# A hybrid mLSTM / attention / MoE step on one core: first projection in two feature halves, context blocks modulated first, one gate wait placed later, one modulation load issued sooner

## The reference

```python
def ada_mod(cvec, w_ada, b_ada):
    m = jax.nn.silu(cvec) @ w_ada + b_ada
    return jnp.split(m[:, None, :], 6, axis=-1)
...
sh1, sc1, g1, sh2, sc2, g2 = ada_mod(c, w_ada[l], b_ada[l])
h = rmsnorm(xs, norm_mix[l]) * (1.0 + sc1) + sh1
q_m, k_m, v_m, o_m, gates, q_d, k_d, v_d = project(h, w_in[l], b_gate[l])
```

## Time and profile before

| | us |
|---|---|
| runs | 775.79, 778.3, 778.33 |
| median | 778.3 |
| profiled execution | 777.91 |
| its span (first to last instruction) | 776.1 |
| TensorE busy in it | 677.3 |
| VectorE busy | 342.4 |
| ScalarE busy | 174.6 |
| GpSimd busy | 103.1 |

### The profile page before, as it was taken

The page is one execution under the profiler, slowest core; times in us unless marked ns, Lnnn a source line. Parts: engine busy times, 40 slices in busy tenths (PEclk is TensorE's granted clock), DMA queues, the critical chain, the costliest instruction groups (busy, mean ns, idle before and its releaser), DMA issues.

```text
span 776.1 us, 7589 instructions
## 1 busy us (share of the span) xinstructions
PE 677.3 (87%) x2660; PEld 364.4 (47%) x2660; DVE 342.4 (44%) x737; ACT 174.6 (23%) x418; POOL 103.1 (13%) x135
## 2 busy tenths in 40 slices
PE   3899999799999999995889989992999999999910
PEld 1344474245555565543667545552544444444400
DVE  2254263131455524468888175667111202111157
ACT  5000200001222111112677412122011211121133
POOL 1222000031101111002451100002111001110040
PEclk9879999999999999998999998996899999999955
DMA  8997423903130130304000386001599999999273
GB/s 292 388 346 256 169 96 105 356 2 136 41 124 14 54 110 14 109 0 164 0 1 1 137 299 269 28 27 61 180 343 359 338 355 356 356 368 346 87 284 136
DMA packets 63027, 137.88 MB, mean 178 GB/s; under 512 B 4647, under 2 KB 11167, under 8 KB 62997
## 3 DMA queue, kind: packets, MB, share of 16 engines
q1 hardware_dynamic: 53064, 112.43, 40.8%
q0 software_dynamic: 5248, 15.63, 5.6%
q10 hardware_dynamic: 4684, 9.44, 3.1%
HBM read 122.70 MB, written 14.74 MB: 177 GB/s over the span
## 4 chain that ended last, share of the span: by engine, by line
PE 75%; DVE 9%; DMA 6%; issue 4%; SPq 3%; ACT 2%; DVEq 0%; POOLq 0%; POOL 0%; ACTq 0%
PE PS L1458 25%; PE PS L1766 14%; PE PS L1644 7%; PE PS L1781 7%; PE PS L1450 5%; DMA PR<-in_w_ada 3%; PE PS L1489 2%; PE PS L1759 1%; PE PS L1633 1%; DVE PR L975 1%; DMA PR<-scratch_mod 1%; PE PS L1563 1%; PE PS L1537 1%; DVE stat L1104 1%; SPq L406 1%
## 5 line engine op out<-in xcount | busy, mean ns | idle before, releaser
L1458 PE MATMUL PS<-RING,hT 128*128 128x512 f32 x480 | 215.8, 598 | 1.3 <-DVE hT L931 1.3
L1458 PEld LDWEIGHTS PS<-RING,hT 128*128 128x128 f32 x480 | 88.7, 192 | 102.7 <-issue 102.2
L1766 PE MATMUL PS<-PR,RING 128*128 128x512 f32 x256 | 113.8, 598 | 0.1
L1644 PE MATMUL PS<-RING,hT 128*128 128x512 f32 x160 | 74.1, 616 | 0.0
L1766 PEld LDWEIGHTS PS<-PR,RING 128*128 128x128 f32 x256 | 47.8, 192 | 55.6 <-issue 53.8
L1781 PE MATMUL PS<-PR,RING 128*128 128x512 f32 x128 | 57.6, 592 | 0.0
L1644 PEld LDWEIGHTS PS<-RING,hT 128*128 128x128 f32 x160 | 30.4, 198 | 33.6 <-issue 33.5
L1319 DVE TENSOR_TENSOR RING<-RING,PS 128x256 f32<-128x256 f32 x16 | 6.7, 422 | 77.8 <-ACT RING L846 77.8
L1314 DVE COPY RING<-PS 128x512 f32<-128x512 f32 x32 | 20.6, 686 | 45.7 <-PE PS L1759 45.2
L1781 PEld LDWEIGHTS PS<-PR,RING 128*128 128x128 f32 x128 | 23.7, 190 | 26.8 <-issue 26.8
L1450 PE MATMUL PS<-hT,RING 128*128 128x512 f32 (+3 forms) x128 | 35.4, 435 | 0.0
(11 more groups left out here) (317 smaller groups left out, 901.7 us busy)
## 6 DMA issues: line engine op xcount, KB each, us to landing
PR<-in_w_gate_up SPq DMA_DIRECT2D x16, 2048.0 KB, 10.5
PR<-in_w_ada SPq DMA_DIRECT2D x20, 1024.0 KB, 13.3
PR<-in_w_down SPq DMA_DIRECT2D x16, 1024.0 KB, 12.5
RING<-in_w_in SPq DMA_DIRECT2D x14, 1024.0 KB, 7.4
scratch_y<-RING ACTq DMA_DIRECT2D x16, 512.0 KB, 7.8
RING<-in_w_ada SPq DMA_DIRECT2D x4, 1024.0 KB, 13.0
RING<-in_w_out SPq DMA_DIRECT2D x4, 1024.0 KB, 6.2
TMP<-scratch_gfr SPq DMA_DIRECT2D x10, 256.0 KB, 4.9
```

Source lines behind the costliest of these rows:

```text
L1458: last = mm(PS[:, m % 2, :], hTv[:, k, t * P:(t + 1) * P], ring[:, ci % 2, k, :], start=(k == 0), stop=(k == KD - 1))
L1644: last = mm(PS[:, i % 4, :], hTv[:, k, t * P:(t + 1) * P], ring[:, (WOUT + q) % 2, k, :], start=(k == 0), stop=(k == KD - 1))
L1766: last = mm(PS[:, 4 + b, :], xgT[:, b, k, :], gub[b][:, k, :], start=(k == 0), stop=(k == KD - 1))
```

## The change

Four things are altered, all in the first part of the program.

1. **Loads.** SP issues the `w_ada` blocks in the order 0, 2, then the first half (features 0 to 511) of the first `w_in` chunk, then blocks 1 and 3, and then the second half of that chunk. Block 1 lies in ring slot 1, block 3 in `TMP`. The ring's chunk 1 ("mq") waits for `ada(1)`.
2. **Order of the projection.** When blocks 0 and 2 are through, VectorE modulates the first four feature blocks, context columns first (`modulate1(0)`), and TensorE runs the first halves of all five "mk" tiles in five PSUM banks (`FIRST_BANK`), with `ada(1)`, `ada(3)` and their columns between them. `modulate1(1)` follows, and the loop over m then runs only the second halves of the first five tiles.
3. **Gate rows.** VectorE's wait for `gate_split`, and the operation that reads the rows, stand behind the second "mk" tile's copy and no longer ahead of the loop.
4. **Late modulation.** Block 9 is loaded right after the store of the gate rows, one chunk sooner.

The diff, cut to its core:

```diff
-CHUNKS = ([("ada", n * 512) for n in range(2)] + [(w, OFF[w]) for w in WIN_ORDER]
-          + [("out", 0), ("out", 512)])
-ADA1, WIN0, WOUT = 0, 2, 9
+CHUNKS = [(w, OFF[w]) for w in WIN_ORDER] + [("out", 0), ("out", 512)]
+WOUT = 7
+FIRST_BANK = (2, 3, 0, 1, 5)
...
-    ada_late = [PR[:, 4096 * i:4096 * (i + 1)].rearrange("p (k n) -> p k n", k=KD) for i in range(2)]
+    ada_w1 = [v.rearrange("p (k n) -> p k n", k=KD) for v in (PR[:, 0:4096], RING[:, 4096:8192], PR[:, 4096:8192],
+                                                              TMP[:, 6676:10772])]
...
-    MB_AFTER = {5: (0, 1), 6: (2, 3), 7: (4, 5, 6), 8: (7, 8, 9)}
+    MB_AFTER = {3: (0, 1), 4: (2, 3), 5: (4, 5, 6), 6: (7, 8, 9)}
...
+        def load_chunk(ci, halves_=(0, 1)):
             kind, col = CHUNKS[ci]
             w = w_dram.get(kind, a["w_in"][0]).rearrange("(h k p) n -> h p k n", h=2, p=P)
-            for hf in range(2):
+            for hf in halves_:
...
-        load_chunk(0)
-        load_chunk(1)
         w_late = a["w_ada"][0].rearrange("(h k p) n -> h p k n", h=2, p=P)
-        for i in range(2):
+
+        def load_ada1(n_):
+            done = (late_in[0], None, late_in[1], ada3_in)[n_]
             for hf in range(2):
-                sp.dma_start(ada_late[i][:, 4 * hf:4 * hf + 4, :],
-                             w_late[hf, :, :, (2 + i) * 512:(3 + i) * 512]).then_inc(late_in[i], 16)
+                sp.dma_start(ada_w1[n_][:, 4 * hf:4 * hf + 4, :], w_late[hf, :, :, n_ * 512:(n_ + 1) * 512]
+                             ).then_inc(half_in[2 + hf] if n_ == 1 else done, 16)
+
+        load_ada1(0)
+        load_ada1(2)
+        load_chunk(0, (0,))
+        load_ada1(1)
+        load_ada1(3)
+        load_chunk(0, (1,))
...
-        for ci in range(2, len(CHUNKS)):
-            kind2, col2 = CHUNKS[ci - 2]
-            if kind2 == "ada":
-                sp.wait_ge(ada_done, col2 // 512 + 1)
+        for ci in range(1, len(CHUNKS)):
+            if ci == 1:
+                sp.wait_ge(ada_done, 3)
             else:
-                sp.wait_ge(mm_done, NT * (WIN_ORDER.index(kind2) + 1))
+                sp.wait_ge(mm_done, NT * (ci - 1))
             load_chunk(ci)
-            if ci == 3:
+            if ci == 1:
                 for n_ in range(4, 8):
                     load_ada2(n_)
-            if ci == 4:
+            if ci == 2:
                 load_ada2(8)
                 sp.wait_ge(gate_step, 2)
                 sp.dma_start(scratch["gfr"], gf.rearrange("p d t -> p (d t)")).then_inc(gf_stored, 16)
-            if ci == 5:
-                for n_ in range(9, 12):
+                load_ada2(9)
+            if ci == 3:
+                for n_ in range(10, 12):
...
-            src = PS[:, m % 2, :]
+            src = PS[:, FIRST_BANK[m] if m < NT else m % 2, :]
...
-        V.memset(gzero, 0.0)
...
-        for n_ in range(4):
-            dve.wait_ge(ada_done, n_ + 1)
-            V.tensor_copy(adp[0:ROWS4 - 1, n_, :], PS[0:ROWS4 - 1, 4 + n_ % 2, :]).then_inc(ada_row, 1)
-        dve.wait_ge(adacol_T, 4)
-        V.tensor_copy(modc[:, 0:8, :], PS[:, 6, 0:16].rearrange("p (k c) -> p k c", c=2))
-        step(V.scalar_tensor_tensor(modc[:, 8:16, :], PS[:, 6, 16:32].rearrange("p (k c) -> p k c", c=2), 1.0,
-                                    cols[:, 16:24].unsqueeze(2).broadcast_to([P, KD, 2]), ALU.add, ALU.mult))
-
-        dve.wait_ge(hraw_a, NT)
-        dve.wait_ge(hraw_v, NT)
-        for k in range(KD):
+        def modulate1(hf):
+
+            for n_ in (hf, 2 + hf):
+                dve.wait_ge(ada_done, 2 * hf + n_ // 2 + 1)
+                V.tensor_copy(adp[0:ROWS4 - 1, n_, :], PS[0:ROWS4 - 1, 4, :]).then_inc(ada_row, 1)
+            ks = slice(4 * hf, 4 * hf + 4)
+            dve.wait_ge(adacol_T, 2 * hf + 2)
+            V.tensor_copy(modc[:, ks, :], PS[:, 6, 8 * hf:8 * hf + 8].rearrange("p (k c) -> p k c", c=2))
+            step(V.scalar_tensor_tensor(modc[:, 8 + 4 * hf:12 + 4 * hf, :],
+                                        PS[:, 6, 16 + 8 * hf:24 + 8 * hf].rearrange("p (k c) -> p k c", c=2), 1.0,
+                                        cols[:, 16 + 4 * hf:20 + 4 * hf].unsqueeze(2).broadcast_to([P, 4, 2]), ALU.add, ALU.mult))
+            if hf == 0:
+                dve.wait_ge(hraw_a, NT)
+                dve.wait_ge(hraw_v, NT)
             for c, (lo, hi) in enumerate(((0, CTX), (CTX, T))):
-                last = V.tensor_scalar(hTv[:, k, lo:hi], hTv[:, k, lo:hi], modc[:, 8 + k, c:c + 1], modc[:, k, c:c + 1],
-                                       ALU.mult, ALU.add)
-            last.then_inc(h_ready, 1)
+                for k in range(4 * hf, 4 * hf + 4):
+                    V.tensor_scalar(hTv[:, k, lo:hi], hTv[:, k, lo:hi], modc[:, 8 + k, c:c + 1], modc[:, k, c:c + 1],
+                                    ALU.mult, ALU.add).then_inc(h_ready, 1)
+
+        modulate1(0)
+        modulate1(1)
+        V.memset(gzero, 0.0)
...
-        dve.wait_ge(gate_split, 64)
-        step(V.scalar_tensor_tensor(ee, gf, -1.0, gf, ALU.mult, ALU.min))
-        dve.sem_inc(gate_step, 1)
...
+            if w == "mk" and t == 1:
+                dve.wait_ge(gate_split, 64)
+                step(V.scalar_tensor_tensor(ee, gf, -1.0, gf, ALU.mult, ALU.min))
+                dve.sem_inc(gate_step, 1)
...
-        ada(0, ADA1)
         xn_T(2)
         xn_T(3)
-        ada(1, ADA1 + 1)
+        ada(0, 0)
         xn_T(4)
         pe.wait_ge(early_loaded, 48)
-        ada_cols(0)
-        ada(2, ADA1 + 2)
-        ada_cols(1)
-        ada(3, ADA1 + 3)
-        ada_cols(2)
-        ada_cols(3)
+        ada_cols(0, 0)
+        ada(2, 1)
+        ada_cols(2, 1)
 
         def gates():
             pe.wait_ge(early_loaded, 48)
+            pe.wait_ge(h_ready, 16)
...
-            ci = WIN0 + c
-            if m >= 2 and hf == 0:
+            ci = c
+            bank = FIRST_BANK[m] if m < NT else m % 2
+            if m >= NT and hf == 0:
                 pe.wait_ge(mm_evac, m - 1)
+            if m < 4 and hf == 0:
+                pe.wait_ge(hraw_a, NT)
+                pe.wait_ge(hraw_v, NT)
...
-                if m == 0:
-                    pe.wait_ge(h_ready, k + 1)
-                last = mm(PS[:, m % 2, :], hTv[:, k, t * P:(t + 1) * P], ring[:, ci % 2, k, :],
+                if m < 2:
+                    pe.wait_ge(h_ready, 8 * hf + 4 * m + k % 4 + 1)
+                last = mm(PS[:, bank, :], hTv[:, k, t * P:(t + 1) * P], ring[:, ci % 2, k, :],
...
+        proj(0, 0)
+        proj(1, 0)
+        ada(1, 2)
+        proj(2, 0)
+        ada_cols(1, 2)
+        ada(3, 3)
+        proj(3, 0)
+        ada_cols(3, 3)
+        proj(4, 0)
         for m in range(ALONE * NT):
             w, t = WIN_ORDER[m // NT], m % NT
-            proj(m, 0)
+            if m >= NT:
+                proj(m, 0)
             proj(m, 1)
```

More of the change, by code:

```diff
@@ L883, in _ @@
         V.memset(stat[:, 60:61], EPS).then_inc(eps_ready, 1)
-        V.memset(PS[:, 4:6, :], 0.0).then_inc(eps_ready, 1)
+        V.memset(PS[:, 4, :], 0.0).then_inc(eps_ready, 1)
         dve.wait_ge(cols_T, 1)
@@ L1385, in halves, with ada_cols @@
         def halves(ci, hf):
-            pe.wait_ge(half_in[2 * (ci % 2) + hf], 16 * (ci // 2 + 1))
+            pe.wait_ge(half_in[2 * (ci % 2) + hf], 16 * (ci // 2 + 1 + ci % 2))
         def ada(n_, ci):
-            if n_ >= 2:
-                pe.wait_ge(ada_row, n_ - 1)
-            w = ring[:, ci % 2] if n_ < 2 else ada_late[n_ - 2]
+            if ci >= 1:
+                pe.wait_ge(ada_row, ci)
             for k in range(KD):
-                if k % 4 == 0:
-                    if n_ < 2:
-                        halves(ci, k // 4)
-                    elif k == 0:
-                        pe.wait_ge(late_in[n_ - 2], 32)
+                if n_ == 1 and k % 4 == 0:
+                    pe.wait_ge(half_in[2 + k // 4], 16)
+                elif k == 0:
+                    pe.wait_ge((late_in[0], None, late_in[1], ada3_in)[n_], 32)
                 g = 32 * (k % 4)
-                last = mm(PS[g:g + 2, 4 + n_ % 2, :], silc[:, k, :], w[:, k, :], start=(k < 4), stop=(k >= 4),
+                last = mm(PS[g:g + 2, 4, :], silc[:, k, :], ada_w1[n_][:, k, :], start=(k < 4), stop=(k >= 4),
                           tile_position=(0, g))
             last.then_inc(ada_done, 1)
-        def ada_cols(n_):
-            pe.wait_ge(ada_row, n_ + 1)
+        def ada_cols(n_, ci):
+            pe.wait_ge(ada_row, ci + 1)
             for j in range(4):
```

2 lines of the change are left out of this document (1 added, 1 removed).

## The result

| | before | after |
|---|---|---|
| median, us | 778.32 (four runs, 775.79 to 779.78) | 768.23 (four runs, 767.73 to 770.41) |
| profiled execution, us | 777.91 | 770.41 |
| its span, us | 776.1 | 768.6 |

The ratio of after to before is 0.9872, with a 95% interval of 0.9853 to 0.9892: faster by 1.3%, 10.1 us of the medians. The forecast was 765.1 (761.5 to 770.5), a gain of 13.2 us. The way and the range were right, and 3 us of the gain are missing.

A forecast was written before the change was run, and what follows sets the result against it. TensorE, busy 677.3 of 776.1 us, was taken to bound the kernel, with time to gain only in its waits and low clock. An earlier start (7.1) plus block 9 sooner (6.1) gave 13.2 us: 765.1 us, range 761.5 to 770.5.

The forecast's parts named there:

- Part 1: Start of the projection: with reordered loads its first matmul runs at 30.0 us, where it was 42.87.
- the clock's variants: Ahead of the projection: `ada(0)` takes 1.83 us at full clock or 3.54 at low; start 29.1 or 30.8 us.
- block 2 at the low level: Start: variant, with its columns, 2.6 us less gain; rival, with `ada(0)` also, 3.4 us less, 768.5 us, chance 0.12.
- Part 2: Projection start to fifth tile's end: 52.1 us of work, ending at 82.1 us instead of 89.2; gain 7.1 us.
- The rival of the five banks: First halves of the projection: the clock stays low throughout, 20.9 us more, 786 us; chance 0.05.
- Part 3: VectorE's later wait on the gate rows: costs nothing in its new place, with 0.5 us to spare on row 5.
- block 6's weights: Late modulation load: issued at 66.7 us, takes 7.2 us, lands at 73.9; margin 2.5 us.
- Part 4: Late modulation: loading block 9 sooner removes 4.36 us idle and 1.7 us of low clock, 6.1 us.
- the sum: Whole kernel: 7.1 + 6.1 = 13.2 us gained, median 778.3 to 765.1; everything behind the fifteenth tile shifts as one.
- a late wait that only moves: Late modulation rival: block 10 or the masks are late instead, gain there 0 to 2 us, 769 to 771 us; chance 0.07.

The follow-up runs named there:

- no_late: Changed kernel with late modulation block 9 loaded at its old place; 771.83 us, ratio to the kernel before 0.9921.
- thin_split: Changed kernel with the thirty four-column gate transposes in three groups of ten, parts of the m = 8 tile between them; 766.28 us, ratio 0.9851.
- again: The changed kernel once more, with no edit; 767.26 us, ratio to the kernel before 0.9851.
- gate_old: Changed kernel with VectorE's wait on the gate rows back ahead of the loop; 771.78 us, ratio to the kernel before 0.9899.
- pairs: Changed kernel with VectorE modulating pair by pair again, not context columns first; 767.79 us, ratio to the kernel before 0.9838.
- delay: Changed kernel with 1.7 us of unneeded dense matmuls ahead of the second block; 767.88 us, ratio to the kernel before 0.9860.
- late_only: Kernel before with one edit, block 9 of the late modulation loaded right behind the store of the gate rows; 771.85 us, ratio 0.9916.
- warm_all: Changed kernel with fills at the start, split gate transposes, and fills ahead of attention transposes, router logits and experts; 761.31 us, ratio 0.9777.

## Why the prediction was right, and where it was off

**Part 1, the start.** Predicted 29.1 or 30.8 us by the clock's variants, taken 30.0. Measured in the profiles with the changed start: 28.8, 28.9, 29.4, 30.3, 30.5 and 31.2 (no_late, thin_split, again, gate_old, after, pairs; delay 31.4). The pieces landed at the forecast pace. Behind the four transposes in a row `ada(0)` took 1.90 us, the full level, in each. What I had only as a variant and in a rival, block 2 at the low level, came in four of the seven instead (2.6 to 3.5 us in after, pairs, gate_old and delay).

**Part 2, to the fifth tile.** Predicted end 82.1 us; 83.6 after, 81.3 again (counted as the 89.20 of the earlier trace rows). The additions were sized right. After has a longer low stretch (9.72 us where 8.97 was taken over from before). The rival of the five banks did not happen: behind 36 us the clock stayed at 1.00 through the first halves in every profile, as in these stretches of the profile after:

```profile
35.00:36.00 1.00, 1.00 (x3) 0.43 (x2) 0.00 (x0) 0.00 (x0) 0.00 (x0) 0.62 1.04 387
36.00:37.00 1.00, 1.00 (x3) 0.38 (x2) 0.00 (x0) 0.00 (x0) 0.00 (x0) 1.00 1.11 397
...
46.00:47.00 1.00, 1.00 (x13) 0.58 (x16) 0.00 (x0) 0.00 (x0) 1.00 (x3) 1.00 1.07 391
```

The Trainium skill, TensorE: Matmul & The Clock Gate, section "A second HAM failure mode: psum-queue depth-cycling", tells of a swing in another kernel. No such swing is in these rows: halves of 3.4 us in five banks, with thin matmuls between, ran at a granted clock of 1.00 from 36 us on.

**Part 3, the gate rows.** The reading operation was to end at 73.0 and row 5 at 75.9, wanted at 76.4, and block 6's weights to come with 2.5 us to spare. VectorE after, as the earlier trace rows:

```profile
72.58 1.47 DVE L996 SCALAR_TENSOR_TENSOR TMP<-TMP 4x1280 f32<-4x1280 f32 x1
74.67 2.12 DVE L920 TENSOR_TENSOR TMP<-PS,TMP 2x512 f32<-2x512 f32 x3 [0.62 <-DVE TMP L996]
76.83 0.69 DVE L921 TENSOR_TENSOR TMP<-PS,TMP 2x512 f32<-2x512 f32 x1
```

The reading operation ended at 74.05 and row 5 at 77.52, and TensorE was ready for block 6 at 77.83 (1.4 us later than forecast, most of it from the start and the low stretch behind it): 0.3 us to spare. The weights had less: TensorE waited 0.23 us for them, ready at 78.06. From the first of their two issues (67.93) they took 10.1 us in place of 7.2; the chain's 9.68 counts from the second. That term was too small. Two loads of 256 KB each for the caches, which POOL issues at 67.79 and 68.36, moved from 70 to 74 us beside them; before, they were issued at 59.95 and 60.52, ahead of the weights at 63.54. Whether they account for all of the 2.9 us isn't shown. A wait of TensorE for a transfer between 60 and 150 us was one of the signs that the forecast named for being wrong; it came, at 0.23 us, in this profile. In the other profiles with the new start nothing waited there that an edit hadn't put back. The price of the old place, 4.5 us, is shown by gate_old.

**Part 4, block 9.** Right in mechanism and size: 6.1 us in late_only, 6.2 between no_late and again. Block 10 was never waited for.

**The step that failed** is the sentence in the sum that everything behind the fifteenth tile "keeps its order and its waits, and shifts as one", and with it the silent assumption that the work between the fifth tile and m = 10 does so too. Order and waits did shift as one (174.7 us in each profile for the mLSTM stage). The clock didn't. It cost 1.7 us at the thin transposes, and what was lost further on is 1.0 in the attention and 1.3 at the router. Delay and thin_split show this for the first. For the attention and the router it is shown that their lengths vary without any edit in them (75.2 to 76.7 and 76.9 to 79.4 us), and for the attention that the length goes with the clock: the six profiles with 6.8 us at the low level there took 75.2 to 75.5 us, the seven with 10.2 to 13.7 took 76.3 to 76.7 (warm_all, with its fill, left out). The router had 22.4 us at the low level before and 24.8 after. What sets the moment in each wasn't settled.

In numbers for "again": 7.9 us from the first two stages (7.1 predicted), 4.4 from the third (6.1), less 1.0 and 1.3, is 10.1 with rounding: the gain of the span.

That the time lies in the range is in part luck. The lower gain was given room for rivals that did not happen (a late wait that only moves set the bound of 770.5), and the loss that did happen, 4.0 us in "again", isn't among them; 0.8 us of it was made up by the first two stages (7.9 us gained, 7.1 forecast).

## What to carry to other kernels

When a change moves work in time, write down which later stretches are thin for TensorE (idle waits, or many matmuls of few columns), and put a microsecond or two of doubt on each (1.0 to 1.7 us at three such places here): their clock is not carried along. Fill a wait that exists anyway with unneeded matmuls, or spread thin ones between wide ones, and look whether another engine's work behind it takes the gain; don't put a fill where the next useful step could already run. And price a wait at the place where it will stand after the change: the same wait was free in the old order and 4.5 us in the new one.
